# Order of work at the attention's entry and at the first downward items of a hybrid decoder step

## Chip, cores and metric

One Trainium2 chip, one of its cores. The metric is the device time of one execution in microseconds (us). TensorE does the matrix products, VectorE (DVE) and ScalarE (ACT) the elementwise work, GpSimd (POOL) issues row fetches and some DMAs, SyncE (SP) issues the other DMAs. The program is written engine by engine: each engine has its own queue of instructions in a fixed order, and engines meet only at counting semaphores. An instruction behind a wait in a queue waits as well.

## What is computed

One decoder layer for a prompt of 512 tokens and 8 samples with one token each. Of the reference, what matters here:

```python
# sample: compressed, selected and window attention over cached pages; prompt: the same three branches
ck, ends = compress(chunk_proj(kv_c, cmp_w[0]), *cmp_w)      # keys and values of 31 compressed blocks
o_c, p_c = dense_attend(q, q_pos, ck[..., 0, :], ck[..., 1, :], ends, rel_bias, None)
o_att = g[:, :, 0] * o_c + g[:, :, 1] * o_s + g[:, :, 2] * o_w
# PEER: for each token 128 rows of two tables of 16384 x 1024
z = jnp.einsum('nd,nhkd->nhk', xc, u_tab[e])
act = (jax.nn.gelu(z.astype(jnp.float32)) * g).astype(xc.dtype)
return jnp.einsum('nhk,nhkd->nd', act, v_tab[e])
```

## The kernel before

**Stages.** Pages of the cache, modulation and the input projection (to about 242 us), attention and the recurrence's output (to about 470), routing of PEER with its queries (to about 680), and then PEER itself, in two halves. The tokens are split there. For 392 tokens (the last 384 of the prompt and the 8 samples) all 16384 experts are computed as dense products: 128 upward items (`up`, L971 to L981: the rows of 128 experts of table u, split by ACT (`high`) and DVE (`low`) into two float32r parts uh and ul, three products for each of eight blocks, 24 matmuls of 392 columns) and 128 downward items (`down`, L1080 on, the same with table v, accumulated in all eight banks of PSUM). For the first 128 tokens, single rows are fetched by index: `dot_rows(n)` (L1809 on) takes the product of the n-th fetched rows of u with the hidden state, 128 times, and `add_rows(n)` (L1978 on) adds the n-th fetched rows of v, weighted by ag, to vacc, 128 times. Both use a ring of four row buffers gb; POOL's fetch of row n waits for the dot (u) or the sum (v) four rows before. The weights of the dense half are built in the chunks of the upward items (`quad`), moved to `stage` by ACT and written to memory by POOL (`store_stage`), one chunk in four pieces of 896 KB; the results of the upward items go to memory (zs) and come back in the downward items as zin.

**Order in the attention's entry.** TensorE (L763 to L925) does: transposes; the scores of the samples' compressed blocks (`strips(2, ...)`, bank 2); waits for the pages; the scores of the selected pages (two `strips`); the new keys; the window's scores; sums for the recurrence's norm (L787); `gsum` (L793 to L796); `hidden_prompt(1)` and `hidden_prompt(0)` (L747), the hidden layer of the prompt's compression for values and keys, 64 products each, recorded as 128 matmuls; the turned probabilities of window (L804, L805), of compressed and selected (L808 to L811), for which it waits for ACT's gelus (gelu_ready 4); the two last products of compression (L814, L815); the window outputs (`outputs(2 * P, ...)`, L824, 80 recorded matmuls); the prompt's compressed scores (L847), which end in pc_s; the selected outputs (L824, 160), which end in sel_free; then turns of the prompt's probabilities (`turn_cached`, L857), the samples' output rows (L866), scores(0), and the loop over 16 units (query tile, branch, pair of heads).

DVE runs the samples' softmaxes (L1559 to L1617), the norm (`inverse_ms`, L1399, and the scaling of zT, L1619), the prompt's compressed softmax (L1657 to L1671, pc_dve 1 before ACT's exp and pc_dve 2 at its end), the sum of the samples' outputs (L1673, L1674), four pairs of copies (`turned`, L1679) and, from `ttr(0)` on (L1630), the units. ttr(0) is the first to need biasT. POOL loads biasT (from rrows) after sel_free; SP loads w_out and x again after sel_free and biasT.

**Order at the end of the upward items.** After the last chunk DVE does dots 118 to 121 and then, for i in 123 to 127, low(i), with two dots behind each of the first three:

```python
for i in range(P - TAIL_U + 1, P):
    low(i)
    for n in range(LAST_G, P)[2 * (i - P + TAIL_U - 1):2 * (i - P + TAIL_U)]:
        dot_rows(n)
```

LAST_G is 122 and TAIL_U 6. Then come gate_item(0), low(128), low_item(0), and the weights ag (a gelu of ACT, issued behind its gelu of item 125, and a product). In each downward item DVE does gate_item (zin times the gates), add_rows, low_item (al, the low part) and low of the next item. up(b) waits for lo_done b + 1; down(k) for lo_done k + 129 and a_ready k + 1. ACT does high(b + 4) behind the gelu of up item b, and in the downward items high_a(k) and the high part of a later item once TensorE is done with the slot. POOL fetches rows 0 to 121 of u, then writes the last stage (four pieces, after QUADS moves of ACT), then fetches rows 122 to 127 of u and all of v; the first four of v wait for dots 124 to 127. SP, in order: store_z(b) and load_raw(b + 8) up to load_raw(130), which waits for low(126); the waits for the stage's stores; load_g(0), load_z(0), and so on. At downward item 8 it loads x (2080 KB) back.

Of the kernel before, what the change touches and what calls it, by code (L numbers as in the profile page):

```python
# [20 lines left out]
P = 128  # L21
# [3 lines left out]
NB = 8  # L25
# [22 lines left out]
NCH = DN // TC  # L48
# [9 lines left out]
CH_U, CH_G = 9, 14  # L58
LAST_G = sum(TILE_G) + NCH * CH_G + 4
TAIL_U = 6  # L60
# [31 lines left out]
def build(nc, io):  # L92
    ctx = ExitStack()
    with ctx:
# [371 lines left out]
        def _(pool):  # L466
# [70 lines left out]
            for n in range(P):  # L537
                if n >= 4:
                    pool.wait_ge(S["ttr_done"], n - 3)
                gather(n, io["u"], n % 4)  # L540
                if n in after_gather:
                    store_stage(*after_gather[n])
                if n == LAST_G - 1:
                    for q in range(PIECES):
                        store_stage(NCH - 1, q)
# [10 lines left out]
        def _(pe):  # L556
# [210 lines left out]
            for br in range(2):  # L767
# [4 lines left out]
            strips(2, slice(0, NCMP_S), lambda b: ckT[:, b * 64:b * 64 + NCMP_S],  # L772
                   ohd[0:33, 31:31 + 16 * (NCMP_S - 1) + 1:16]).then_inc(S["att_pe"], 1)
            pe.wait_ge(S["pages_sync"], 16 * 50)
            pe.wait_ge(S["pages_pool"], 16 * 46)
# [18 lines left out]

            pe.wait_ge(S["w1v_loaded"], 32)
            pe.wait_ge(S["mt_done"], ADA_ALL)  # L796
            hidden_prompt(1, 7, 128)
            pe.wait_ge(S["w1k_loaded"], 64)
# [19 lines left out]
            def outputs(first, parts):  # L818

                for a in range(2):  # L820
# [6 lines left out]
                return last  # L827
            pe.wait_ge(S["win_loaded"], 16)
            pe.wait_ge(S["att_dve"], 4)
            outputs(2 * P, [(10, NB, lambda b: vnew[0:NB, 1, :])] +  # L830
                    [(11 + kb, P, lambda b, kb=kb: vwin[:, b * 4 + kb, :]) for kb in range(4)])

# [11 lines left out]
            for i in range(4):  # L844
                for r in range(GRP):
                    for g in range(2):
# [4 lines left out]
                           [(2 + kb, P, lambda b, kb=kb: sel[:, b * 8 + kb, P:2 * P]) for kb in range(8)])  # L851
            last.then_inc(S["sel_free"], 1)


# [43 lines left out]

            pe.wait_ge(S["pc_tdone"], 4)
            for i in range(4):  # L900
                for q in range(4):
                    u = 4 * i + q
                    if u < 15:
                        scores(u + 1)
                    if q == 0 and i >= 2:
                        pe.wait_ge(S["o_done"], i - 1)
                    if q % 2 == 0:
                        cols = slice(q * P, (q + 2) * P)
                        for g in range(2):
                            mm(ps[half(g), 6 + i % 2, cols], vc[0:NCMP_P, 8, half(g)],  # L910
                               ptcb[0:NCMP_P, i, g * 512:(g + 1) * 512][:, cols], start=True, stop=False)
                    apply(u)
# [209 lines left out]
        def _(act):  # L1122
# [223 lines left out]
            for b in range(P - TAIL_U, P):  # L1346
                if b == P - 1:
                    high_a(0)
                gelu(b, b % 4)
                if b == P - 3:  # L1350
                    act.wait_ge(S["ttr_done"], P)
                    fn(ag[:, :], zg[:, :], ACT.Gelu_apprx_tanh).then_inc(S["zg_gelu"], 1)

            for k in range(P):
                if k >= 4:
                    act.wait_ge(S["pe_item"], P + k - 3)
                if k >= 1:
                    high_a(k)
# [9 lines left out]
        def _(dve):  # L1368
# [248 lines left out]
            inverse_ms(512, 4)  # L1617
            dve.wait_ge(S["rstd_ready"], 2)
            link(*[stt(zT[:, c, :], zT[:, c, :], par[:, NLG + c:NLG + c + 1], rstd, MUL, MUL) for c in range(4)])  # L1619

# [40 lines left out]
            link(tt(pcb, pcb, pcm[:, 0, :].to_broadcast([P, 4 * NH, NCMP_P]), SUB))  # L1661
            dve.sem_inc(S["pc_dve"], 1)
            dve.wait_ge(S["pc_exp"], 1)
            link(dve.tensor_reduce(pcm[:, 1, :], pcb, AX.X, ADD))
# [6 lines left out]
            dve.sem_inc(S["pc_dve"], 1)  # L1671
            dve.wait_ge(S["sel_free"], 1)
            link(cp(osb.rearrange("p a b -> p (a b)"), ps[:, 1, 0:2 * P]))  # L1673
# [7 lines left out]
            turned(0)  # L1681
            dve.wait_ge(S["os_ready"], 1)
            grp = []
# [6 lines left out]
            turned(1)  # L1690
            turned(2)
            dve.wait_ge(S["lru_stored"], 32)
            dve.sem_inc(S["lru_dve"], 1)
            dve.wait_ge(S["bias_loaded"], 16)
            ttr(0)
            turned(3)
            for i in range(4):
# [248 lines left out]
            for n in range(QUADS):  # L1946
# [5 lines left out]
                for q in after_quad(i, CH_G):  # L1952
                    dot_rows(sum(TILE_G) + ch * CH_G + q)
            for n in range(LAST_G - 4, LAST_G):
                dot_rows(n)
# [11 lines left out]
            for i in range(P - TAIL_U + 1, P):  # L1967
                low(i)
                for n in range(LAST_G, P)[2 * (i - P + TAIL_U - 1):2 * (i - P + TAIL_U)]:
                    dot_rows(n)  # L1970
            gate_item(0)
            low(P)
            low_item(0)
            dve.wait_ge(S["zg_gelu"], 1)
            link(tt(ag[:, :], ag[:, :], gwt[:, :], MUL))


            def add_rows(n):  # L1978
# [4 lines left out]
                else:  # L1983
                    dve.wait_ge(S["acc_step"], n)
                    stt(vacc[:, :], gb[:, n % 4, :], ag[:, n:n + 1], vacc[:, :], MUL, ADD).then_inc(S["acc_step"], 1)  # L1985
            for k in range(P):
                if k:
                    gate_item(k)
                add_rows(k)
                if k:  # L1990
# [140 lines left out]
```

## Time and profile before

| | us |
|---|---|
| median of 3 runs | 1822.7 (1821.66 to 1826.14) |
| the profiled execution | 1822.52 |
| its span in the trace | 1820.0 |
| TensorE busy | 1746.2 (96%) |
| DVE busy | 1314.0 (72%) |
| ACT busy | 647.6 (36%) |
| POOL busy | 341.5 (19%) |
| mean granted clock of TensorE | 0.974 of full speed |

The profile is of one execution. Its page gives busy times, the chain of work that ended last (followed back from the last instruction to what released each one) and the costliest groups. Times of matmuls are those of a pipeline: a busy TensorE is not one at its peak, and what counts is the distance between starts. "Granted clock" is the part of 2.4 GHz that the throttle let through; it has two levels, 1.2 and 2.4 GHz. An idle time stands with the instruction that ended it, and with what released that instruction; "issue" names time in which no wait is seen. A stage is read from its own stretch: the engines' timelines there, the chain, and the windows with the DMA's rate.

### The profile page before, as it was taken

The numbers are of one execution on the slowest core, as the hardware profiler recorded it, in microseconds if no ns is written. First come the engines' busy times: TensorE is split into PE (matmuls) and PEld (weight loads), VectorE is DVE, ScalarE is ACT, GpSimd is POOL, SyncE is SP. The second block draws the span as 40 slices with busy tenths as digits, with TensorE's granted clock in tenths as the row PEclk, the third lists the DMA queues.
The fourth block names the chain that finished last, engine by engine and source line by source line (L and its number), as shares of the span: only waits on it lengthen the run. The fifth ranks groups of instructions, "written<-read, shape, count | busy, mean of one in ns | idle before, by whom it ended". The sixth has DMA issues, their size and how long they took to land.

```text
span 1820.0 us, 30382 instructions
## 1 busy us (share of the span) xinstructions
PE 1746.2 (96%) x11385; PEld 1626.7 (89%) x11385; DVE 1314.0 (72%) x2978; ACT 647.6 (36%) x1023; POOL 341.5 (19%) x372
## 2 busy tenths in 40 slices
PE   7999998779899999999999999998999999999997
PEld 5688876448799999999999999998999999999997
DVE  0224336662676799998999999956787777777776
ACT  1114422661332234343333333332343333333332
POOL 3101000000000002111333333333222222222220
PEclk9999986899899999999999999998999999999999
DMA  9767654300532147776899999989999999999992
GB/s 345 245 220 278 223 162 161 119 1 1 185 126 85 70 129 270 246 234 205 288 364 365 365 348 339 336 314 371 403 395 330 340 342 335 340 339 330 345 309 78
DMA packets 178952, 467.85 MB, mean 257 GB/s; under 512 B 20515, under 2 KB 92707, under 8 KB 177294
## 3 DMA queue, kind: packets, MB, share of 16 engines
q1 hardware_dynamic: 130974, 290.20, 45.9%
q0 software_dynamic: 45120, 173.61, 26.4%
q10 hardware_dynamic: 2736, 2.49, 0.4%
q8 instruction: 68, 1.11, 0.2%
q14 instruction: 54, 0.44, 0.1%
HBM read 408.86 MB, written 64.17 MB: 260 GB/s over the span
## 4 chain that ended last, share of the span: by engine, by line
PE 85%; DVE 6%; DMA 4%; ACT 2%; issue 1%; ACTq 1%; SPq 0%; POOL 0%; DVEq 0%
PE ps L1089 28%; PE ps L979 25%; PE ps L716 6%; PE ps L966 5%; PE ps L1068 5%; PE ps L919 3%; PE ps L618 2%; ACT arena L1132 1%; PE ps L591 1%; DMA xT<-in_u,gidx 1%; DMA arena<-in_w_in 1%; PE ps L895 1%; PE ps L887 1%; DMA raw<-in_v 1%; DVE arena L1630 1%
## 5 line engine op out<-in xcount | busy, mean ns | idle before, releaser
L1764 DVE TENSOR_TENSOR ul<-raw,uh 128x1024 fp32r<-128x1024 f32 x256 | 311.5, 1222 | 117.8 <-ACT uh L1132 116.3
L979 PE MATMUL ps<-hh,uh 128*128 128x392 f32 x1024 | 358.2, 350 | 8.7 <-DVE ul L1764 8.7
L979 PE MATMUL ps<-hl,uh 128*128 128x392 f32 x1024 | 349.8, 342 | 0.0
L979 PE MATMUL ps<-hh,ul 128*128 128x392 f32 x1024 | 349.0, 341 | 0.0
L1089 PE MATMUL ps<-ah,uh 128*128 128x392 f32 x1000 | 339.6, 340 | 2.5 <-DVE al L1966 2.5
L1089 PE MATMUL ps<-ah,ul 128*128 128x392 f32 x1000 | 341.7, 342 | 0.0
L1089 PE MATMUL ps<-al,uh 128*128 128x392 f32 x1000 | 340.9, 341 | 0.0
L1132 ACT ACTIVATE uh<-raw 128x1024 fp32r<-128x1024 f32 x256 | 269.8, 1055 | 105.6 <-PE ps L1089 91.2
L523 POOL DMA_INDIRECT xT<-in_u,gidx x128 | 148.8, 1163 | 585.6 <-DVE zg L1812 370.1
L523 POOL DMA_INDIRECT xT<-in_v,gidx x128 | 132.4, 1034 | 408.7 <-DVE vacc L1985 388.4
L1132 ACT ACTIVATE zbuf<-ps 128x392 f32<-128x392 f32 x128 | 63.7, 498 | 407.0 <-PE ps L979 407.0
L979 PEld LDWEIGHTS ps<-hh,uh 128*128 128x128 f32 x1024 | 193.3, 189 | 10.9 <-DVE ul L1764 9.3
L979 PEld LDWEIGHTS ps<-hl,uh 128*128 128x128 f32 x1024 | 193.3, 189 | 0.0
L979 PEld LDWEIGHTS ps<-hh,ul 128*128 128x128 f32 x1024 | 193.2, 189 | 0.0
L1089 PEld LDWEIGHTS ps<-ah,uh 128*128 128x128 f32 x1000 | 187.9, 188 | 3.2 <-issue 1.9
L1089 PEld LDWEIGHTS ps<-al,uh 128*128 128x128 f32 x1000 | 187.8, 188 | 0.0
L1089 PEld LDWEIGHTS ps<-ah,ul 128*128 128x128 f32 x1000 | 187.7, 188 | 0.0
L1812 DVE CUSTOM_DVE_ANT_0 xT<-xT,hg 128x1024 f32<-128x1024 f32 x128 | 155.2, 1215 | 22.7 <-DMA xT<-in_u,gidx 22.5
L1985 DVE SCALAR_TENSOR_TENSOR vacc<-xT,ag,vacc 128x1024 f32<-128x1024 f32 x127 | 162.3, 1278 | 0.0
L1132 ACT ACTIVATE ah<-zin 128x392 fp32r<-128x392 f32 x128 | 68.2, 532 | 236.9 <-DVE zin L1962 236.9
L716 PE MATMUL ps<-arena 128*128 128x260 f32 x576 | 132.5, 389 | 2.9 <-DVE arena L1418 2.0
L716 PEld LDWEIGHTS ps<-arena 128*128 128x128 f32 x576 | 109.2, 192 | 20.1 <-DMA arena<-in_w_in 3.1
(355 smaller groups left out, 2221.1 us busy)
## 6 DMA issues: line engine op xcount, KB each, us to landing
raw<-in_uT SPq DMA_DIRECT2D x128, 512.0 KB, 5.1
raw<-in_v SPq DMA_DIRECT2D x128, 512.0 KB, 6.3
zs<-zbuf SPq DMA_DIRECT2D x128, 196.0 KB, 5.3
gw<-stage POOLq DMA_DIRECT2D x28, 896.0 KB, 8.9
gr<-gw SPq DMA_DIRECT2D x32, 784.0 KB, 8.3
zin<-zs SPq DMA_DIRECT2D x128, 196.0 KB, 5.8
arena<-in_ada_w SPq DMA_DIRECT2D x32, 512.0 KB, 4.4
arena<-in_w_in SPq DMA_DIRECT2D x18, 512.0 KB, 6.8
```

The costliest lines, as they stand in the source:

```text
L523: pool.indirect_dma_start(out=gb[:, s, :], out_offset=None, in_=table, in_offset=bass.IndirectOffsetOnAxis(ap=gidx[:, n:n + 1], axis=0)).t ...
L618: last = mm(ps[g * HD:(g + 1) * HD, 2 + 2 * c + h, 1 - m:257 - m], w1p[:, c * 16 + m * 8 + j, :], xv[:, h, :, c, g, j, :], start=(m == 0 a ...
L716: last = mm(ps[:, 2 * (n % 2) + h, 0:HALF], win_w[:, (n % 2) * KD + k, :], hT[:, k, h * HALF:(h + 1) * HALF], start=(k == 0), stop=(k == K ...
L919: last = mm(ps[:, 2 + 2 * (c % 3) + h, 0:HALF], wout[:, k, c * P:(c + 1) * P], zT[:, k, h * HALF:(h + 1) * HALF], start=(k == 0), stop=(k ...
L966: last = mm(ps[:, b + h, 0:HALF], weights[w](k), moving[m](k)[:, h * HALF:(h + 1) * HALF], start=(first and n == 0 and w == 0 and m == 0), ...
L979: last = mm(ps[:, bank, 0:DN], w[x][:, k * P:(k + 1) * P], m[:, k, G0:TOK], start=(k == 0 and x == 0 and m is hh), stop=(k == KD - 1 and x ...
L1068: last = mm(ps[:, 4 + n % 4, t * P:(t + 1) * P], oh[:, n % 6, t * P:(t + 1) * P], oh[:, n % 6, (4 + t) * P:(5 + t) * P], start=True, stop= ...
L1089: last = mm(ps[:, dc, 0:DN], w[:, q, cols], m[:, q, :], start=(first and w is uh and m is ah), stop=False)
L1132: return act.activation(out, in_, f, **kw)
L1764: tt(ul[:, i % 4, :], raw[:, i % 4, :], uh[:, i % 4, :].bitcast(F32), SUB).then_inc(S["lo_done"], 1)
L1812: dve.tensor_tensor_reduce(gb[:, n % 4, :], gb[:, n % 4, :], hg[:, :], 1.0, 0.0, MUL, ADD, zg[:, n:n + 1]).then_inc(S["ttr_done"], 1)
L1985: stt(vacc[:, :], gb[:, n % 4, :], ag[:, n:n + 1], vacc[:, :], MUL, ADD).then_inc(S["acc_step"], 1)
```

## The change

Five moves; no product and no transfer is added or removed.

- TensorE: the values' part of the prompt's compression (hidden_prompt(1), with its two waits) goes from behind gsum to between the samples' compressed strips and the wait for the pages.
- TensorE: the window outputs go behind the selected outputs, and so behind the prompt's compressed scores; they count os_ready, for which DVE waits in the place of sel_free. The wait for pc_tdone 4 goes behind scores(1).
- DVE: the scaling of zT goes behind pc_dve 1; ttr(0) goes ahead of turned(2).
- DVE: dots 122 to 127 go from the last upward items to downward items 0 to 5. add_rows starts at item 6, and items 19, 39, 59, 79, 99 and 119 do two.
- ACT and DVE: the gelu and the product that make ag go to downward item 6. LATE_G is 6; P - LATE_G is what LAST_G was.

```diff
-LAST_G = sum(TILE_G) + NCH * CH_G + 4
+LATE_G = P - sum(TILE_G) - NCH * CH_G - 4
@@ tensor
             strips(2, slice(0, NCMP_S), lambda b: ckT[:, b * 64:b * 64 + NCMP_S],
                    ohd[0:33, 31:31 + 16 * (NCMP_S - 1) + 1:16]).then_inc(S["att_pe"], 1)
+            pe.wait_ge(S["w1v_loaded"], 32)
+            pe.wait_ge(S["mt_done"], ADA_ALL)
+            hidden_prompt(1, 7, 128)
             pe.wait_ge(S["pages_sync"], 16 * 50)
             pe.wait_ge(S["pages_pool"], 16 * 46)
...
-            pe.wait_ge(S["w1v_loaded"], 32)
-            pe.wait_ge(S["mt_done"], ADA_ALL)
-            hidden_prompt(1, 7, 128)
             pe.wait_ge(S["w1k_loaded"], 64)
             hidden_prompt(0, 1, 160)
...
-            pe.wait_ge(S["win_loaded"], 16)
-            pe.wait_ge(S["att_dve"], 4)
-            outputs(2 * P, [(10, NB, lambda b: vnew[0:NB, 1, :])] +
-                    [(11 + kb, P, lambda b, kb=kb: vwin[:, b * 4 + kb, :]) for kb in range(4)])
...
             last.then_inc(S["sel_free"], 1)
+            pe.wait_ge(S["win_loaded"], 16)
+            last = outputs(2 * P, [(10, NB, lambda b: vnew[0:NB, 1, :])] +
+                           [(11 + kb, P, lambda b, kb=kb: vwin[:, b * 4 + kb, :]) for kb in range(4)])
+            last.then_inc(S["os_ready"], 1)
...
-            pe.wait_ge(S["pc_tdone"], 4)
             for i in range(4):
                 for q in range(4):
                     u = 4 * i + q
                     if u < 15:
                         scores(u + 1)
+                    if u == 0:
+                        pe.wait_ge(S["pc_tdone"], 4)
@@ scalar
-                if b == P - 3:
-                    act.wait_ge(S["ttr_done"], P)
-                    fn(ag[:, :], zg[:, :], ACT.Gelu_apprx_tanh).then_inc(S["zg_gelu"], 1)
             for k in range(P):
                 if k >= 4:
                     act.wait_ge(S["pe_item"], P + k - 3)
+                if k == LATE_G:
+                    act.wait_ge(S["ttr_done"], P)
+                    fn(ag[:, :], zg[:, :], ACT.Gelu_apprx_tanh).then_inc(S["zg_gelu"], 1)
                 if k >= 1:
                     high_a(k)
@@ vector
             inverse_ms(512, 4)
-            dve.wait_ge(S["rstd_ready"], 2)
-            link(*[stt(zT[:, c, :], ...) for c in range(4)])
...
             dve.sem_inc(S["pc_dve"], 1)
+            dve.wait_ge(S["rstd_ready"], 2)
+            link(*[stt(zT[:, c, :], ...) for c in range(4)])
             dve.wait_ge(S["pc_exp"], 1)
...
-            dve.wait_ge(S["sel_free"], 1)
+            dve.wait_ge(S["os_ready"], 1)
...
-            dve.wait_ge(S["os_ready"], 1)
+            dve.wait_ge(S["os_ready"], 2)
...
             turned(1)
-            turned(2)
             dve.wait_ge(S["lru_stored"], 32)
             dve.sem_inc(S["lru_dve"], 1)
             dve.wait_ge(S["bias_loaded"], 16)
             ttr(0)
+            turned(2)
             turned(3)
...
             for i in range(P - TAIL_U + 1, P):
                 low(i)
-                for n in range(LAST_G, P)[2 * (i - P + TAIL_U - 1):2 * (i - P + TAIL_U)]:
-                    dot_rows(n)
             gate_item(0)
             low(P)
             low_item(0)
-            dve.wait_ge(S["zg_gelu"], 1)
-            link(tt(ag[:, :], ag[:, :], gwt[:, :], MUL))
...
+            def added(k):
+                def rows_until(m):
+                    return max(m - LATE_G, 0) + min(m // 20, LATE_G)
+                return range(rows_until(k), rows_until(k + 1)) if k >= LATE_G else ()
             for k in range(P):
                 if k:
                     gate_item(k)
-                add_rows(k)
+                if k < LATE_G:
+                    dot_rows(P - LATE_G + k)
+                if k == LATE_G:
+                    dve.wait_ge(S["zg_gelu"], 1)
+                    link(tt(ag[:, :], ag[:, :], gwt[:, :], MUL))
+                for n in added(k):
+                    add_rows(n)
                 if k:
                     low_item(k)
```

## Rows read from the trace of the kernel before

**Rows 1.** the page: chain by engine, and the group of add_rows
```profile
PE 85%; DVE 6%; DMA 4%; ACT 2%; issue 1%; ACTq 1%; SPq 0%; POOL 0%; DVEq 0%
...
L1985 DVE SCALAR_TENSOR_TENSOR vacc<-xT,ag,vacc 128x1024 f32<-128x1024 f32 x127 | 162.3, 1278 | 0.0
```
**Rows 2.** chain in order of time, 240 to 312: start us, us, what
```profile
275.99 4.89 PE ps L824 x80
280.88 6.97 PE ps L847 x64
287.85 7.70 PE ps L824 x160
...
295.83 8.82 DMA arena<-rrows
```
**Rows 3.** timelines of TensorE, ACT and DVE, 250 to 310: start us, us, engine line
```profile
256.98 4.39 PE L747 MATMUL ps<-arena 64*64 64x31 f32 x143
262.35 5.98 PE L747 MATMUL ps<-arena 64*64 64x31 f32 x113 [0.99 <-issue]
...
270.47 0.48 PE L808 MATMUL ps<-ident,arena 128*63 128x64 f32 x2
...
263.82 1.15 ACT L1132 ACTIVATE arena<-arena,cst 128x1032 f32<-128x1032 f32 x1 [7.21 <-DVEq L1603]
...
266.38 0.60 ACT L1132 ACTIVATE arena<-ps,posb 64x31 f32<-64x31 f32 x2
...
280.83 2.77 DVE L1619 SCALAR_TENSOR_TENSOR arena<-arena,par 128x520 f32<-128x520 f32 x4 [0.70 <-ACT arena L1132]
...
305.72 1.27 DVE L1679 COPY arena<-ps 31x512 f32<-31x512 f32 x2
307.53 0.18 DVE L1639 RECIPROCAL cst<-cst 128x4 f32<-128x4 f32 x1 [0.53 <-ACT arena L1132]
```
**Rows 4.** busy time in stretches: us, then each engine, PEclk, DMA share, GB/s
```profile
260.00:264.00 4.00, 3.01 (x84) 2.90 (x80) 3.48 (x8) 0.18 (x1) 0.00 (x0) 0.83 0.68 182
292.00:296.00 4.00, 3.50 (x92) 2.21 (x84) 2.71 (x6) 1.03 (x1) 0.17 (x1) 0.83 0.01 4
304.00:308.00 4.00, 0.89 (x8) 0.90 (x8) 2.69 (x14) 1.65 (x8) 0.00 (x0) 0.88 0.69 224
```
**Rows 5.** chain in order of time, 1205 to 1315
```profile
1207.46 4.30 PE ps L979 x24
...
1214.01 2.18 POOL gw L531 x4
...
1216.49 12.69 DMA xT<-in_u,gidx
...
1242.71 9.50 DMA zin<-zs
...
1252.31 0.57 DVE zin L1962
...
1254.64 34.56 PE ps L1089 x192
```
**Rows 6.** timelines of DVE and of TensorE, 1225 to 1240
```profile
1229.20 1.22 DVE L1812 CUSTOM_DVE_ANT_0 xT<-xT,hg 128x1024 f32<-128x1024 f32 x1 [15.54 <-DMA xT<-in_u,gidx]
...
1232.89 0.70 PE L979 MATMUL ps<-hh,uh 128*128 128x392 f32 x1 [7.37 <-DVE ul L1764]
```
**Rows 7.** chain, and timeline of TensorE, about item 13
```profile
1291.19 15.77 DMA raw<-in_v
...
1311.51 0.45 PE L1089 MATMUL ps<-ah,uh 128*128 128x392 f32 x1 [0.91 <-DVE al L1966]
```
**Rows 8.** busy time in stretches of the downward entry and of the steady part
```profile
1214.00:1254.00 40.00, 31.65 (x161) 30.99 (x159) 13.37 (x19) 9.87 (x15) 15.32 (x14) 0.87 0.94 354
1254.00:1311.00 57.00, 55.96 (x312) 55.62 (x312) 44.23 (x56) 18.58 (x25) 13.85 (x13) 1.00 1.04 402
1360.00:1780.00 420.00, 420.00 (x2354) 420.00 (x2353) 330.63 (x392) 156.02 (x197) 98.87 (x98) 1.00 0.95 334
```

More of the change, by code:

```diff
@@ L542, in _ @@
                     store_stage(*after_gather[n])
-                if n == LAST_G - 1:
+                if n == P - LATE_G - 1:
                     for q in range(PIECES):
@@ L1617, in _ @@
             inverse_ms(512, 4)
-            dve.wait_ge(S["rstd_ready"], 2)
-            link(*[stt(zT[:, c, :], zT[:, c, :], par[:, NLG + c:NLG + c + 1], rstd, MUL, MUL) for c in range(4)])
             def ttr(u):
@@ L1662, in _ @@
             dve.sem_inc(S["pc_dve"], 1)
+            dve.wait_ge(S["rstd_ready"], 2)
+            link(*[stt(zT[:, c, :], zT[:, c, :], par[:, NLG + c:NLG + c + 1], rstd, MUL, MUL) for c in range(4)])
             dve.wait_ge(S["pc_exp"], 1)
@@ L1953, in _ @@
                     dot_rows(sum(TILE_G) + ch * CH_G + q)
-            for n in range(LAST_G - 4, LAST_G):
+            for n in range(P - LATE_G - 4, P - LATE_G):
                 dot_rows(n)
```

## The prediction

> **What bounds the kernel now.** I read the page first: TensorE is on 85% of the chain that ended last [rows 1], so a change pays only where TensorE, or what releases it, gets through its queue sooner. The chain in order of time leaves TensorE in two places that the change edits. In the attention's entry TensorE works with hardly a wait to 295.55; then the chain is a DMA of 8.82 us, the load of biasT, and DVE's ttr(0) behind it at 304.7 [rows 2]. At the end of the upward items the chain goes through a row fetch of 12.69 us and, after another fetch, a load of z of 9.50, and reaches the first downward matmul at 1254.64 [rows 5]. The engines' timelines say why: DVE stood 15.54 us before dot 122 with low(124) behind it in its queue, and TensorE stood 7.37 us before up(124) [rows 6], after which it also ran at a low clock for a while (mean granted clock 0.87 from 1214 to 1254 [rows 8]). The downward items are then even, eight in 34.56 us, 4.32 each [rows 5], but for one stall of 0.91 at item 13 (1311.51) [rows 7].
>
> **Entry: compression, strips, outputs.** Nothing is added or removed on TensorE. hidden_prompt(1), 128 small matmuls, goes ahead of the other strips: 4.39 us for 143 [rows 3], so 3.9. Strips 0 and 1 waited for nothing (no gap stands between them and the ones before), so there is no hole for it to fill; everything up to gsum, and with it DVE's chain of sample softmaxes, comes 3.9 later. ACT's third exp then starts at 267.7 instead of 263.82 and lasts 1.15; a table load follows it (the gelus start 1.4 after its end), and the four gelu pieces, two in 0.60, are all ready by then: gelu_ready 4 at 271.5. TensorE waits for that before L808, which stood at 270.47: 1.0 later [rows 3]. Before it TensorE idles some 4 us, which cost nothing by themselves.
>
> From L808 on I keep the low clock of these rows: it is granted 0.83 of full speed in 260 to 264 and again in 292 to 296, and 1.2 GHz, the lower level, between [rows 4]. L808 to L815 take 5.4, to 277.0. The window outputs (4.89) are no longer here. The prompt's scores (6.97) end at 284.1 instead of 287.85, the selected outputs (7.70) at 291.8 [rows 2], and sel_free comes 3.8 earlier. In POOL's queue only the load of biasT stands behind it: 0.3 + 8.82 later, at 300.9, ttr(0) can start. SP's loads of w_out and x, behind the same semaphores, move as much forward; nobody is near waiting for them. The window outputs now run under the load of biasT, 3 to 4.9 us, to 296 at latest.
>
> On DVE the scaling of zT (2.77 [rows 3]) leaves a hole before the prompt's scores and goes between pc_dve 1 and pc_exp, where ACT's exp hides about 1.2 of it: +1.6 on pc_dve 2, which comes near 295, as TensorE finishes the window outputs. The turns and copies behind it, four pairs of copies of 1.27 each [rows 3], took from 297 to 304, with the old load as their cover; now they end near 301, but for two pairs, turned(2) and turned(3), behind ttr(0). Before, one pair stood there, and DVE waited 0.53 for ACT after it; so +0.7. Entry in sum: 3.8 - 0.7 = **3.1 us gained**. The wait on pc_tdone behind scores(1) lets those matmuls run under the copies; the cached outputs still wait for the last copy, so this is inside the 3.1. From there to 1203 the order is the same and the shift passes through. Bounds: 1.5, if the turns last longer and biasT isn't what ends last; 7, if the clock stays high over L811 to L847, half of some 12 us at 1.2 GHz.
>
> **Downward entry.** Dots 122 to 127 leave the tail, so DVE does low(124) to low(127) as ACT delivers. One up item takes 4.30 [rows 5], a low 1.2: nothing stands before up(124) at 1225.5, and four items end at 1242.7. The first downward item also needs the gates and zin(0). SP issues their loads behind load_raw(130), which waits for low(126), now at 1224, and for the stage's stores, issued from 1214.01 [rows 5], landing near 1227. With 9.50 for the landing zin(0) is there at 1237.5. A bound from bytes: ahead of it stand 3.7 MB of stage, 2.1 of rows and 3.7 in SP's queue, 9.5 MB at 402 GB/s [rows 8] from 1214: 1237.7, or 1239.7 with the slow start. gate, low(128) and low_item(0), as wide as the gate, add 0.57 + 1.2 + 0.57 [rows 5]: 1240 to 1242, under the last up item. First downward matmul at 1243 instead of 1254.64: 11.6.
>
> The DMA takes part of it back. From 1254 to 1311 it moved 402 GB/s, all engines busy, against 334 in the steady part [rows 8]; TensorE's stall at item 13 comes from raw rows that landed at 1306.96 after 15.77 us, behind x coming back [rows 7]. Bytes from 1214 to that landing: 40 x 0.354 + 53 x 0.402 = 35.5 MB. Its rows being six behind, the change asks for 6 x 0.52 = 3.15 MB less by then: 32.3 MB, 80.4 us at 0.402, and 1.7 for the slow start, so landed at 1296.1 and item 13 at 1300.6. TensorE alone would be there at 1243 + 13 x 4.32 = 1299.2. So the stall grows to some 2 us and the gain at item 13 is 1311.5 - 1300.6 = **10.9 us**.
>
> The six dots (1.22 [rows 6]) stand in items 0 to 5 in the place of add_rows (1.28 [rows 1]): nothing. The gelu of ag and its product, an eighth of a dot's width each, come at item 6, under 0.3 each as an estimate; behind ACT's wait for dot 127 is high_a(6), and both engines are some two items ahead of TensorE there. The six extra add_rows, one each 20 items, stand before low_item and low. Over 98 steady items DVE is busy 330.63 of 420 [rows 8], idle 0.91 per item, and its lead covers the rest; without the lead 6 x 0.4 = 2.2 us. POOL's fetches of v start six items later, in step with DVE. The last add_rows keeps its place.
>
> **The sum.** The profiled execution took 1822.5 (span 1820.0), 0.2 below the median 1822.7; I let that go. 1822.5 - 3.1 - 10.9 = 1808.5.
>
> The page "DMA: Bandwidth & Descriptors" of the Trainium skill (Where 436 GB/s comes from) gives about 358 GB/s per core as the bound for transfers between HBM and SBUF. By that figure the 32.3 MB would take 90 us and leave about 1 us of gain at item 13, an estimate from that page. The trace moved 402 over 57 us, nearly all such transfers, so the measurement decides.
>
> **Rivals.** A measurement of this kernel can tell about 0.3%, 5.5 us, from no change.
> 1. The DMA takes more back. At the 354 GB/s of 1214 to 1254 [rows 8] the 32.3 MB would be 91.2 us, item 13 at 1309.7, gain 1.8, time 1817.6. Against it: that rate holds the slow start and DVE's late dots, after which POOL had nothing to fetch. The full case 0.05; something between, to 1813 or 1815, 0.08.
> 2. The entry gives nothing or costs up to 2: the later gelus move more than I see, or code is fetched late again (a hole of 0.99 that no wait explains [rows 3]): 1811.5 to 1813.5. Chance 0.12.
> 3. The clock is kind: it fell near 307 after a stretch in which TensorE did 0.89 us in 4 [rows 4]; scores(1) and less idling stand there now. If it stays high over the small units, or over L811 to L847, 4 to 6 us more: 1803 to 1804.5. Chance 0.15.
> 4. Slower than before: late rows. A slot of gb is fetched again only when its dot or add is done, so a landing may take four items, 17.2 us, before it holds DVE, and a_ready with it. The longest row fetch here took 12.69 [rows 5]. Beyond 17.2 each us costs a quarter per item, 5 us over the some 20 saturated items: from 17.2 + 14 / 5 = 20 us on, nothing is left of the gain, and at 22 it is 1832. For it: the DMA is saturated, raw rows took 15.77. Against: those stood in SP's queue, and fewer rows are wanted. Chance 0.03.
> 5. It doesn't do what it says: TensorE stops at up(124) all the same, for raw rows behind the stores or for zin(0) at 1248, and half of the 10.9 comes back: 1813 to 1814. Chance 0.05.
> The forecast, 1805 to 1811.5: 0.52.
>
> **Numbers.** Predicted 1808.5. About 0.07 below 1803 and 0.10 above 1815.5 are left out: 1803 to 1815.5. Faster by more than 5.5 us, under 1817.2: all but the full case of 1 and 4, 0.91. Within 5.5: 0.06. Slower: 0.03.
>
> **What would show it.** Right: no idle of TensorE from 1203 to item 0; first downward matmul 14 to 16 us before 1254.64; a stall of 1 to 3 us near item 13, with the DMA at 400 GB/s around it; sel_free near 292, biasT landed near 301; L808 near 271.5 with 4 us of idle before it. Wrong: sel_free no earlier; TensorE waiting for zin(0) or for rows in items 0 to 12; TensorE stopping where two add_rows stand together; steady items above 4.29.

## The result, and the profile after

| | before | changed |
|---|---|---|
| median (lowest to highest) of 8 runs each, us | 1820.49 (1814.34 to 1826.45) | 1810.60 (1807.19 to 1815.69) |
| profiled execution, us | 1822.5 | 1809.7 |
| its span, us | 1820.0 | 1807.2 |

The ratio is 0.9944, with a 95% interval from 0.9925 to 0.9963: 9.9 us faster between the medians, where 14 were forecast (ratio 0.9923). The time lies inside the forecast's range, 2.1 above its centre, 1808.5; part of that nearness is the kernel before, whose eight runs have a median 2.0 below the 1822.5 that the forecast's sum started from. A later set of runs of the same kernel gave 0.9937 (0.9917 to 0.9957). The two halves did not share the gain as forecast: the downward half gave more than its term, and the entry gave nothing that can be measured.

The page of the changed kernel: the chain by engine (against [rows 1]), and the two groups of row operations on DVE.
```profile
PE 85%; DVE 7%; DMA 4%; ACT 2%; issue 1%; ACTq 1%; SPq 0%; POOL 0%; DVEq 0%
...
L1981 DVE SCALAR_TENSOR_TENSOR vacc<-xT,ag,vacc 128x1024 f32<-128x1024 f32 x127 | 162.5, 1279 | 0.6
L1813 DVE CUSTOM_DVE_ANT_0 xT<-xT,hg 128x1024 f32<-128x1024 f32 x128 | 155.4, 1216 | 4.9 <-DMA xT<-in_u,gidx 4.8
```
TensorE is still 85% of the chain, and an add_rows lasts as long as before. The idle time before all 128 dots together is 4.9 us; before, one stop alone was 15.54 [rows 6].

**The downward entry.** The chain of the changed kernel in order of time, 1205 to 1330 (start us, us, what), against [rows 5] and [rows 7]:
```profile
1206.35 4.30 PE ps L980 x24
...
1212.91 1.65 POOL gw L531 x3
1214.55 16.05 DMA gw<-stage
...
1231.05 8.66 DMA zin<-zs
...
1239.81 0.57 DVE zin L1963
...
1242.13 34.65 PE ps L1090 x192
...
1277.55 16.32 DMA raw<-in_v
...
1298.42 31.71 PE ps L1090 x176
```
No row fetch stands in it any more. It runs through the stage's stores and zin(0), and the first downward matmul starts at 1242.13, 12.51 before its old start [rows 5]. Some 1.1 of that is no gain of this stretch: in this profile the last chunk and its stores already come 1.1 earlier (stores at 1212.91, before 1214.01). Eight items still take 34.65. DVE's timeline over the same entry (in brackets the idle time before the instruction, and what ended it):
```profile
1217.34 1.23 DVE L1765 TENSOR_TENSOR ul<-raw,uh 128x1024 fp32r<-128x1024 f32 x1 [3.73 <-ACT uh L1133]
1221.64 1.23 DVE L1765 TENSOR_TENSOR ul<-raw,uh 128x1024 fp32r<-128x1024 f32 x1 [3.07 <-ACT uh L1133]
1225.92 1.22 DVE L1765 TENSOR_TENSOR ul<-raw,uh 128x1024 fp32r<-128x1024 f32 x1 [3.06 <-ACT uh L1133]
1239.81 0.57 DVE L1963 TENSOR_TENSOR zin<-zin,gr 128x392 f32<-128x392 f32 x1 [12.66 <-DMA zin<-zs]
```
The lows come as ACT delivers, one in 4.3 us. DVE still stands 12.66 us, but now all upward lows lie behind it, and TensorE has items to do meanwhile. TensorE's timeline shows no idle row from 1203 to the first downward matmul, and from there to 1330 these two:
```profile
1242.13 0.41 PE L1090 MATMUL ps<-ah,uh 128*128 128x392 f32 x1 [0.55 <-DVE al L1967]
...
1298.42 0.45 PE L1090 MATMUL ps<-ah,uh 128*128 128x392 f32 x1 [0.24 <-DVE al L1967]
```
The stall at item 13 is there, but it shrank from 0.91 [rows 7] to 0.24. The view by stretches (us, then busy time and instructions of TensorE, its weight loads, DVE, ACT and POOL, granted clock, DMA share, GB/s), against [rows 4] and [rows 8]:
```profile
292.00:296.00 4.00, 3.17 (x80) 2.28 (x68) 3.58 (x7) 0.00 (x0) 0.68 (x1) 1.00 0.61 182
304.00:308.00 4.00, 1.76 (x8) 0.91 (x8) 2.26 (x13) 2.81 (x12) 0.00 (x0) 0.75 1.04 436
...
1214.00:1254.00 40.00, 39.45 (x221) 39.00 (x220) 17.87 (x25) 13.20 (x19) 10.15 (x11) 1.00 1.03 395
1254.00:1311.00 57.00, 56.76 (x318) 56.44 (x317) 44.51 (x57) 20.78 (x29) 13.25 (x13) 1.00 1.04 403
```
Over these 40 us the DMA is full (395 GB/s, before 354), and TensorE's clock stays at its upper level (1.00, before 0.87).

**The attention's entry.** TensorE's timeline of the changed kernel, and ACT's last exp and gelus there, against [rows 3]:
```profile
240.68 1.07 PE L766 MATMUL ps<-ident,arena 128*128 128x128 f32 x8
...
242.62 4.09 PE L747 MATMUL ps<-arena 64*64 64x31 f32 x128
...
270.99 0.47 PE L808 MATMUL ps<-ident,arena 128*63 128x64 f32 x2 [5.50 <-ACT arena L1133]
...
283.92 10.23 PE L824 MATMUL ps<-arena 63*32 63x128 f32 x240
...
306.47 1.11 PE L887 MATMUL ps<-ident,arena 128*128 128x128 f32 x4 [1.19 <-ACT arena L1133]
...
267.17 1.15 ACT L1133 ACTIVATE arena<-arena,cst 128x1032 f32<-128x1032 f32 x1 [8.18 <-DVEq L1604]
...
269.73 1.22 ACT L1133 ACTIVATE arena<-ps,posb 64x31 f32<-64x31 f32 x4
```
Then its chain, against [rows 2], and a line of DVE's timeline:
```profile
284.00 7.48 PE ps L824 x160
291.76 8.99 DMA arena<-rrows
```
```profile
300.78 0.29 DVE L1629 CUSTOM_DVE_ANT_0 arena<-ps,arena 128x128 f32<-128x128 f32 x1 [0.38 <-DMA arena<-rrows]
```
hidden_prompt(1) runs in 4.09 without a hole, L808 waits 5.50 for ACT's gelus, the load of biasT is issued at 291.76 in the place of 295.83, and ttr(0) starts at 300.78. In this profile the entry went as forecast up to here. What it is worth needs more than one profile, since these stretches differ between executions. The table below takes the starts of four instructions in each profile: the entry's first transposes (L766), L808, ttr(0), and the first transposes of the small units (L887), and gives the times between them.

| profile | L766 at | to L808 | to ttr(0) | to L887 |
|---|---|---|---|---|
| before | 241.38 | 29.09 | 34.21 | 4.65 |
| changed | 240.68 | 30.31 | 29.79 | 5.69 |
| e1_down_only | 246.78 | 29.17 | 33.97 | 4.66 |
| e2_entry_only | 245.57 | 34.04 | 31.64 | 5.69 |
| e3_compression_only | 244.18 | 36.13 | 35.24 | 4.65 |
| e4_no_compression | 244.71 | 27.44 | 31.56 | 5.69 |
| e5_entry_kv_late | 240.62 | 30.28 | 29.79 | 5.68 |
| e6_after_kv_late | 245.00 | 30.26 | 29.79 | 5.69 |
| e7_stores_behind_rows | 247.03 | 29.59 | 34.69 | 4.66 |
| e8_after_again | 247.57 | 37.23 | 29.79 | 5.68 |
| e9_no_compression_kv_late | 244.76 | 26.72 | 29.78 | 5.70 |
| e10_entry_without_compression | 247.46 | 29.19 | 31.50 | 5.69 |
| e11_x_back_late | 244.72 | 30.27 | 29.79 | 5.68 |
| e12_before_kv_late | 240.73 | 26.27 | 31.03 | 4.66 |

From the end of TensorE's last quad (the last matmuls of L1069, ahead of the last upward items) to the end of the span it is 594.6 to 595.7 us in the seven profiles with the downward half, and 607.1 to 608.7 in the six that have neither it nor e7's order. The averages, 595.1 and 607.8, are **12.7** apart. Within it, from the quad to the first downward matmul it is 30.1 to 30.6 against 40.8 to 42.0.

### The profile page after: what moved, and what is told of

Read it like the earlier page. It is cut to its first block, busy times and chain, and to the rows that moved or that the text cites. A ratio compares the mean times of both kernels' runs of the same rounds, so it can differ in the third digit from the quotient of the medians.

```text
span 1807.2 us, 30381 instructions
## 1 busy us (share of the span) xinstructions
PE 1739.4 (96%) x11385; PEld 1620.2 (90%) x11385; DVE 1314.4 (73%) x2978; ACT 647.6 (36%) x1023; POOL 345.7 (19%) x372
## 4 chain that ended last, share of the span: by engine, by line
PE 85%; DVE 7%; DMA 4%; ACT 2%; issue 1%; ACTq 1%; SPq 0%; POOL 0%; DVEq 0%
PE ps L1090 28%; PE ps L980 25%; PE ps L716 6%; PE ps L967 5%; PE ps L1069 5%; PE ps L920 3%; PE ps L618 2%; ACT arena L1133 2%; PE ps L895 1%; PE ps L591 1%; DMA arena<-in_w_in 1%; PE ps L887 1%; DMA raw<-in_v 1%; DMA gw<-stage 1%; DVE arena L1629 1%
## 5 line engine op out<-in xcount | busy, mean ns | idle before, releaser
L523 POOL DMA_INDIRECT xT<-in_v,gidx x128 | 138.0, 1078 | 377.5 <-DVE vacc L1981 355.2
```

The lines of the kernel that those rows point to most:

```text
L523: pool.indirect_dma_start(out=gb[:, s, :], out_offset=None, in_=table, in_offset=bass.IndirectOffsetOnAxis(ap=gidx[:, n:n + 1], axis=0)).t ...
```

## Experiments

All ran against the kernel before, in 5 rounds; ratios have their 95% interval. None of them leaves anything out of the computation. The names of the parts are those of the diff above.

### The halves, and the compression alone

e1_down_only keeps of the change the downward half: the dots in items 0 to 5, add_rows from item 6, the gelu of ag and its product.

> The downward half alone (dots 122 to 127 in downward items 0 to 5, add_rows from item 6), entry as before. Theory: the gain is TensorE's stop at up(124) and nothing else, so it stands without the entry's half: first downward matmul 11.4 us earlier counted from the last upward item before it (36.1 us in the changed kernel from the matmul at 1206.35, 47.2 before), time 10 to 12 us below the kernel before. Rival: the mean gain of 9.9 is shared evenly, the profiled pair flatters this half, and it gives 6 to 8 us.

Measured: 1811.12 against 1823.23, ratio **0.9932** (0.9909 to 0.9955). The whole gain of the change is in this half, and the even share, the rival, is out.

e2_entry_only is the other half: everything of the diff that is about TensorE, and DVE down to turned(3).

> The entry half alone (compression up, window outputs behind the selected ones, the scaling of zT and ttr(0) moved), upward and downward items as before. Theory: 2 to 3 us are won at the first unit (its turn after scores to start 2.2 earlier, counted from the first sample strip) and the units after it run at a clock that differs from run to run, so that -1 to +2 us are lost again: time 0 to 3 us below before. Rival A (my prediction): the shift passes through, 3.1 us. Rival B: the longer units are caused by the change (TensorE idles 1.5 to 2.4 us more before the first of them) and the half is worth nothing.

Measured: 1826.46, ratio **1.0018** (0.9999 to 1.0038). The entry's half is no gain, and rather a loss. In its profile the first unit (L887) comes 71.4 behind L766 where it came 68.0 behind before, so the 2.2 that were expected there are not won.

e3_compression_only moves hidden_prompt(1) and nothing else of the entry:
```diff
             strips(2, slice(0, NCMP_S), ...).then_inc(S["att_pe"], 1)
+            pe.wait_ge(S["w1v_loaded"], 32)
+            pe.wait_ge(S["mt_done"], ADA_ALL)
+            hidden_prompt(1, 7, 128)
...
-            pe.wait_ge(S["w1v_loaded"], 32)
-            pe.wait_ge(S["mt_done"], ADA_ALL)
-            hidden_prompt(1, 7, 128)
```

> Only hidden_prompt(1) moved up, all else as before. Theory: it fills no hole and delays DVE's and ACT's chain of the samples' softmaxes by 3.9 us, so TensorE idles some 5.5 us before L808 and everything from there on is 0.5 to 1.2 us later; time 0 to 1.5 us above before. Rival: the clock, which now stays high for hidden_prompt(0), rises sooner afterwards and gives 2 us or more back.

Measured: 1827.28, ratio **1.0024** (1.0004 to 1.0044): slower. TensorE's timeline in its profile:
```profile
246.12 3.57 PE L747 MATMUL ps<-arena 64*64 64x31 f32 x114
...
252.14 0.60 PE L747 MATMUL ps<-arena 64*64 64x31 f32 x14 [2.46 <-issue]
```
and by stretches:
```profile
248.00:252.00 4.00, 1.69 (x56) 1.57 (x53) 0.00 (x0) 0.38 (x2) 0.00 (x0) 1.00 0.98 344
252.00:256.00 4.00, 3.86 (x34) 1.18 (x37) 0.00 (x0) 0.00 (x0) 0.00 (x0) 0.68 0.28 107
256.00:260.00 4.00, 4.00 (x24) 0.59 (x16) 0.00 (x0) 0.00 (x0) 0.00 (x0) 0.50 0.57 151
```
The 114th matmul of hidden_prompt(1) is followed by a hole of 2.46 us that no semaphore wait explains, while the DMA is full (0.98). e3's time is above the 0 to 1.5 us that were expected. Behind it the granted clock falls to 1.2 GHz (0.50) over the strips. e2's profile shows both as well, and what the clock does to one strip (mean granted clock 0.76 and 0.82 around it), which lasts 1.92 at full clock:
```profile
253.07 0.60 PE L747 MATMUL ps<-arena 64*64 64x31 f32 x14 [2.02 <-issue]
253.60 3.24 PE L759 MATMUL ps<-arena 128*32 128x512 f32 x16
```
L808 is 34.0 (e2) and 36.1 us (e3) behind L766 in the place of 29.1. The profile of the changed kernel above happened to have no such hole.

e4_no_compression is the changed kernel with hidden_prompt(1) back in its old place, e3's edit in reverse.

> The changed kernel with hidden_prompt(1) back behind gsum. Theory: selected outputs end (sel_free) and biasT starts 0.5 to 1.2 us earlier than in the changed kernel, counted from the first sample strip; time within 2 us of the changed kernel, if anything 1 below (1809.6 where that is 1810.6). Rival: the move up is what makes the entry work, and without it the time is 2 us or more above the changed kernel's.

Measured: 1809.76, ratio **0.9932** (0.9907 to 0.9958). Taking the compression's move out costs nothing that can be measured. L808 stands 27.4 behind L766, and ttr(0) 59.0, 1.1 sooner than in the changed kernel's profile (60.1).

### What makes the hole

The hole's candidates were the DMA traffic beside hidden_prompt(1), and the place alone. While it runs, SP's queue moves the compression weights (two of 512 KB) and then stores o_kv (1560 KB), which nobody waits for. e5_entry_kv_late is e2 with this store moved behind SP's loads of w_out and x, e6_after_kv_late the changed kernel with the same edit:
```diff
             sp.wait_ge(S["z_moved"], ZC)
-            load(io["o_kv"], zT[:, KC:ZC, :], S["kv_stored"])
...
             load(xT[:, :, :], io["xT"], S["x_loaded"])
+            load(io["o_kv"], zT[:, KC:ZC, :], S["kv_stored"])
```

> The entry half alone, as in e2, with SP's store of the new keys and values (o_kv, 1560 KB) moved from just before the entry to behind the loads of w_out and x. Theory: TensorE's hole of 2.0 to 2.5 us at the 114th matmul of hidden_prompt(1), which no wait explains, is code that arrives late because the DMA is full of this store and of cmp_w's load, and the low clock behind it follows from the hole. Without the store the hole is below 0.5 us and the strips behind it run at the high clock: from the first transposes to L808 30 to 31 us instead of 34.0, time 3 to 4.5 us below e2's, so 0 to 2 us below before. Rival: the hole belongs to the place in the code and is there whatever the DMA does; then 34 us and e2's time.

Measured: 1823.44, ratio **1.0009** (0.9992 to 1.0026).

> The changed kernel with the same later store of o_kv. Theory: from the first transposes to L808 30 to 31 us in each profile, time 0 to 4 us below the changed kernel's, by how often that has the hole. Rival: no difference.

Measured: 1811.96, ratio **0.9937** (0.9917 to 0.9957).

e8_after_again is the changed kernel once more, unedited, beside them.

> The changed kernel unchanged, for a second profile and more times. Theory: the entry shows either no hole in hidden_prompt(1), as in the first profile (30.3 us from the first transposes to L808), or one of 2 us or more with a low clock behind it (34 us), as in e2 and e3; from the end of the last chunk to the first downward matmul 35.8 us as before. Rival: always 30.3, and e2's hole has another cause.

Measured: 1811.34, ratio **0.9937** (0.9917 to 0.9957); its profile has the hole, 2.21 us, and the low clock behind it (L808 37.2 behind L766). e5's and e6's profiles have none; e5's timeline of TensorE:
```profile
242.54 4.08 PE L747 MATMUL ps<-arena 64*64 64x31 f32 x128
...
270.90 0.47 PE L808 MATMUL ps<-ident,arena 128*63 128x64 f32 x2 [5.51 <-ACT arena L1133]
```
With the store early, three of five profiles with the compression moved (e2, e3, e8) have the hole, and two (the changed kernel, e11) do not; with it late, none of two. Two profiles are too few to say that the store makes the hole in this order, and a full DMA alone does not make it: in the changed kernel's profile and in e11's the share was 0.97 to 1.04 all through hidden_prompt(1), without a hole. In the times the edit did nothing that these intervals can show: e6 equals e8, e5's 1.0009 and e2's 1.0018 lie in each other's interval. The profiles may show the hole more often than the runs have it: e8's profiled execution, 1822.63, was the slowest of its twelve, and e2's and e3's lay 3.8 and 6.5 above their medians. And without the hole L808 still comes 30.3 behind L766, waiting 5.5 for ACT.

### Order alone at the downward entry

e7_stores_behind_rows is the kernel before, with POOL's last stage stores behind fetch 125 instead of behind 121, so that dots 122 and 123 needn't wait for rows behind 3.7 MB. The theory it tests: the stop came from that order in POOL's queue, and the deferred dots as such add nothing.
```diff
-                if n == LAST_G - 1:
+                if n == LAST_G + 3:
```

> The kernel before, with nothing of the change but POOL's order: the last stage's four stores stand behind the fetch of row 125 of u instead of behind row 121, so that rows 122 to 125 are on their way 6 to 9 us earlier and not behind 3.7 MB. Theory (the stop of 7.4 us at up(124) came from those rows, and nothing else there costs): TensorE's stop at up(124) shrinks to 0 to 2 us; zin(0), behind the stores, still comes at about the same distance from them, so 8 to 11 of the 12 us that the downward half gave come back: time 8 to 11 below before. Rival: the DMA is the bound, so the bytes in front of the downward items only change places, and the gain is below 5 us because this kernel keeps the six rows that the change defers.

Measured: 1818.83, ratio **0.9974** (0.9960 to 0.9989), a third of the half's gain; of these 4.6 us its profile has 2.8 from the quad to the end (605.0 for 607.8). Its chain and its TensorE timeline, 1215 to 1260:
```profile
1221.82 2.19 POOL gw L531 x4
...
1224.32 19.77 DMA xT<-in_u,gidx
...
1248.60 7.44 DMA zin<-zs
```
```profile
1247.78 0.69 PE L979 MATMUL ps<-hh,uh 128*128 128x392 f32 x1 [6.16 <-DVE ul L1764]
...
1258.46 0.41 PE L1089 MATMUL ps<-ah,uh 128*128 128x392 f32 x1 [0.47 <-DVE al L1966]
```
The stop did not go; it moved on to row 126, whose fetch takes 19.77 right behind the same stores (it is issued 2.50 after they begin; the fetch of 12.69 was issued 2.48 after), and TensorE stops 6.16 before up(126) where it stopped 7.37 [rows 6]; the first downward matmul comes 38.3 behind the quad in the place of 42.0. That theory fell: rows have to be taken out from in front of the lows, not only put ahead of the stores.

### The two remaining parts of the entry, and x

e9_no_compression_kv_late joins what e4 and e6 suggest: the changed kernel, hidden_prompt(1) in its old place, the o_kv store late.

> The changed kernel with hidden_prompt(1) back behind gsum and the later store of o_kv. Theory: no hole in hidden_prompt; from the first transposes to ttr(0) 58 to 59 us (60.1 in the changed kernel without the hole, 65.7 and 67.0 with it, 59.0 in e4), the downward half as before; time 1 to 4 us below the changed kernel's. Rival: the hole comes back at another place of the code, 59 us or more.

Measured: **1806.40** (1804.61 to 1807.09) against 1825.37, ratio **0.9893** (0.9874 to 0.9913). This beats both kernels. From L766 to ttr(0) it is 56.5 us, less than the 58 to 59 expected, although a hole of 0.44 stays behind the 143rd matmul. The DMA share in that hole was 0.00.

e10_entry_without_compression is e2 without the move of hidden_prompt(1): the window outputs, the scaling, the turns.

> The entry half without the compression's move, upward and downward items as before. Theory: the moves behind L808 are worth 4.2 us up to ttr(0) and cost 1.0 from there to the first unit (two pairs of copies instead of one), so 59 us from the first transposes to ttr(0) instead of 63.2, and 1 to 3.5 us below before. Rival: this half is worth nothing even without the compression's move, because the units behind it lose what it won.

Measured: 1823.56, ratio **0.9995** (0.9978 to 1.0013). The rival, nothing even without the compression's move, can't be told from this. In its profile ttr(0) comes 60.7 behind L766, not 59: sel_free stands behind the first 160 of the 240 products of L824, and these ran longer at the low clock (0.50 to 0.58 from 268 to 300) than in the changed kernel's profile (9.51 us for 7.48; 12.37 for 10.23 with all 240):
```profile
289.59 12.37 PE L824 MATMUL ps<-arena 63*32 63x128 f32 x240
```

e11_x_back_late is the changed kernel with x coming back behind item 40 (`if k == 8:` becomes `if k == 40:`), to see whether the stall at item 13 comes from it.

> The changed kernel with the load of x (2080 KB) at downward item 40 instead of 8. Theory: the stall at item 13 (0.5 us in the changed kernel's first profile) comes from raw rows behind this load; without it no matmul of the downward items waits, and time is 0 to 1 us below the changed kernel's. Rival (the DMA bound that I used to size the stall): the DMA is short of bytes over the whole stretch, and a stall of the same size comes at another item.

Measured: 1813.61, ratio **0.9930** (0.9904 to 0.9955). TensorE's timeline from 1215 to 1330 has a single idle row:
```profile
1244.34 0.41 PE L1090 MATMUL ps<-ah,uh 128*128 128x392 f32 x1 [0.20 <-DVE al L1967]
```
The stall at item 13 is gone: it was raw rows behind x's load. But there was only 0.24 us of it to gain, and the time can't be told from e8's.

e12_before_kv_late is the kernel before with the late store and nothing else.

> The kernel before with nothing but the later store of o_kv. Theory: hidden_prompt's hole falls from 1.0 to below 0.5 us and the low clock comes no sooner, so from the first transposes to L808 27 to 28.5 us instead of 29.1; time 0.5 to 2.5 us below before. So the 1.1% of e9 is 12 us of the downward half, 2 to 3 of the moves behind L808 and the rest this store. Rival: the store alone gives 4 us or more, and the entry's moves are worth nothing.

Measured: 1817.79 against 1822.48, ratio **0.9977** (0.9963 to 0.9991), 4.7 us faster from one store. Its TensorE timeline, against [rows 3]:
```profile
256.33 7.66 PE L747 MATMUL ps<-arena 64*64 64x31 f32 x256
...
267.00 0.47 PE L808 MATMUL ps<-ident,arena 128*63 128x64 f32 x2 [1.77 <-ACT arena L1132]
```
The 256 matmuls of both hidden_prompts take 7.66 in one piece. Before, they took 11.35 (256.98 to 268.33, from [rows 3]): 4.39, a hole of 0.99, and 5.98 for the rest at a low clock. The gain is above the 0.5 to 2.5 expected, and it is the rival's: the store alone gives over 4 us. Its other half, that the entry's moves are worth nothing, is not contradicted either: the ratios of e1 and e12 multiply to 0.9909, e9 has 0.9893, and 0.9909 lies in its interval. The profiled execution, 1813.20, is the fastest of its twelve, so the 6.0 us that the table has from L766 to L887 (68.0 and 62.0) are more than the median shows.

## Why the prediction was right, and where not

**The downward entry: right, its term too small.** Forecast 10.9; e1's ratio is 12.4 us of 1823.2, and the profiles say 12.7. The steps held: up(124) no longer waits, and the first downward matmul is 11.4 nearer to the quad on the average of the profiles, for 11.6. zin(0) landed at 1239.7, the same number as the second of the two bounds, but by other terms: the stage's stores landed at 1230.6 for 1227, and zin(0) took 8.66 for 9.50. What failed is the term "**the DMA takes part of it back**", 0.7 of the 11.6. From the quad to item 13, in the six profiles without the downward half and the five with it that show a wait there, the averages are 98.9 and 86.7 us: 12.2 gained, so nothing was taken back. The byte count was good: in the changed kernel the raw rows landed 81.0 us behind the start of the stores (1212.91 to 1293.87), at 396 GB/s 32.1 MB, for 32.3 forecast. The forecast gave this 82.1 us, with the rate of 402 and 1.7 for a slow start; measured, the slow start is about 0.5 shorter and the bytes are 0.5 us fewer. So the rows landed 1.1 sooner than forecast, and the stall was 0.24 instead of some 2 (the forecast's own two times, 1300.6 and 1299.2, give 1.4). The four upward items kept the clock as well. The other 0.5 of the 12.7 lies behind item 13, where TensorE's timeline shows no wait for al in either kernel of the pair; no run says what it is. Two of the forecast's signs failed for these reasons and the entry's: the stall of 1 to 3 us, and a first downward matmul 14 to 16 us earlier.

The page "DMA: Bandwidth & Descriptors" of the Trainium skill (Where 436 GB/s comes from), by whose figure of about 358 GB/s only 1 us would have been left at item 13, does not bind in this stretch: the trace shows 403 GB/s over 57 us, and the measurement decides. The section makes its figure by dividing a memory stack's rate by two cores; this program runs on one core, and no run here shows what a second one beside it would do.

**The six deferred adds: right.** add_rows in pairs shows nowhere on TensorE; no idle row stands at them.

**The entry: wrong.** Forecast 3.1 gained; e2 has 1.0018, e10 0.9995, e5 1.0009. This is rival 2, at its 0.12. The steps that failed are "**1.0 later**" for L808, the price of moving the compression, and "**the shift passes through**".

1. Without a hole L808 came 30.3 behind L766 (the changed kernel, e11) against 29.1: 1.2 later, as forecast, waiting 5.5 for gelus that stand behind DVE's sample softmaxes. But in three of five profiles with the store early the compression at its new place has a hole of 2.0 to 2.5 us, and L808 comes at 34.0 to 37.2, 5 to 8 later than before; the rest of the delay, some 2 to 5, is the clock behind the hole. The average of the five is 33.6, that of the five with the compression in its old place (before, e1, e4, e7, e10) 28.9.
2. Behind L808, to ttr(0), six profiles with the new order have 29.8, 4.4 less than before (forecast 3.8 + 1.0). Three (e2, e4, e10) have 31.5 to 31.6, only 2.6 to 2.7 less, where the 240 products of L824 took 12.2 to 12.5 for 9.6 to 10.3 in the others. From ttr(0) to the units it is 1.04 later (forecast 0.7).
3. The small units behind L887, up to the first matmul of L919 (L920 in the changed kernel), last 99.2 to 100.9 us in nine profiles with the new turns and 98.5 to 100.7 in five with the old ones. The averages are 0.8 apart, the ranges overlap, and no run separates the two.

From L766 to that first matmul of L919 the old order takes 167.0, 166.3 and 169.6 us (before, e1, e7). The whole new entry takes 166.5 and 165.0 without a hole, 171.1 and 173.2 with it (e2, e8); without the compression's move it takes 165.4 and 166.5 (e4, e10). So a good execution wins about 2 us and one with the hole loses 3 to 6. The times agree with a sum near nothing. But e5, whose one profile has no hole, should then win 2, and its interval, down to 1.5 faster, just excludes that: how the sum comes to nothing there stays open.

The profile before also hid what the move costs when nothing disturbs the old order. Its 29.1 up to L808 held a hole and a low clock, and I took it as the work's own length. With the store late (e12) the old order needs 26.3, and the moved compression 30.3 (e5, e6): 4.0 more, the compression's own time, 3.9. Behind L808, 3.2 of the 34.2 us before were the clock as well: the old order with a late store takes 31.0, the new one 29.8, and the two late turns give 1.0 of these 1.2 back.

So with the store late the old entry reaches the units 62.0 us behind L766 (e12), the new one without the compression's move 62.2 (e9), and the new one with it 65.8 (e5). That e9 beats the changed kernel agrees: by 4 to 5 us against the latter's two medians, 1810.6 and 1811.3, and by 7 against e11 beside it, which differs from the changed kernel in x alone. The profiled pair itself shows a gain of 2.2 us at L887, and loses 1.6 of it again over the small units, where the clock fell at 304 to 308 (0.75) and lay low longer than before.

**Rival 1**, the DMA taking more back, did not come: the rate from 1214 on was 395 to 403 GB/s, not 354. **Rival 3**, the kind clock, didn't come; the clock was rather unkind where a hole stood. **Rival 4**, late rows: no row fetch held the first items. e7's 19.77 us shows that a fetch can take so long, right behind 3.7 MB of stores. **Rival 5** didn't come. So the total is partly luck. The two errors have opposite signs, +1.8 downward and about -3.1 at the entry, and cancel in part. The gain between the medians, 9.9, is 4.1 short of the 14 forecast; the time is only 2.1 off because the kernel before came out 2.0 faster than the forecast's base.

What stays open: that the hole is TensorE's instructions arriving late is an inference. It stands after a fixed count of matmuls (114 in the new order, 143 in the old) and no semaphore ends it. With the compression in its old place five of five profiles with the store early have a hole of 0.84 to 1.26 us; of the two with it late, e12 has none and e9 one of 0.44, with the DMA idle in it. That the store's place matters is shown by e12's time. That the hole comes from the store beside it is likely and not shown, and what TensorE waits for was not seen.

## What to carry to other kernels

When operations that need data late in a saturated stretch stand in an in-order queue ahead of what the bound engine needs, defer them past it; putting their loads first only moves the stop. Before moving work into a place that looks free, find out how long the stretch is without its holes and its low clock, and look at the DMA share of the new place. And try the place of a store that nobody waits for by itself: here it was worth 4.7 us alone, and with the change 1.1% together.

## What was not expected of the hardware

- TensorE stopped for 0.4 to 2.5 us in a run of small matmuls without any semaphore wait, always behind the same count of them (114 of the new order, 143 of the old). Each of the holes over 2 us (2.02, 2.46, 2.21) stood beside a DMA share of 0.97 or more, but two profiles had this share without a hole, and the one of 0.44 stood beside a share of 0.00. The holes over 2 us were followed by a low granted clock over the next strips (down to 0.76 in e2, 0.50 in e3 and e8): 3.24 us for 16 matmuls of 128x512 that take 1.92. The clock cost about as much as the hole, or more: L808 came 3.7 to 6.9 later than without a hole.
- Two executions of identical code differ by up to 7 us before the entry is reached: L766 starts between 240.6 and 247.6 in fourteen profiles, whose programs are the same up to there. Single profiles of a few us' difference can only be compared stretch by stretch.
- The DMA kept 403 GB/s for 57 us with loads, stores and row fetches mixed. A row fetch right behind 3.7 MB of stores landed after 12.69 us in the kernel before [rows 5] and after 19.77 in e7. At the rates of these stretches, 414 and 391 GB/s, the DMA moved 5.3 and 7.7 MB meanwhile, so more than the stores stood before the second.
